# Two attention branches in halves of the array, and two layer boundaries rearranged, in a three-layer fp32 kernel

## The reference

```
first block:  h = rms_norm(x)*w;  proj = h @ w_in
              o_a = g0*o_cmp + g1*o_slc + g2*o_win     # 8 heads of 64 in 2 key-value groups;
                                                       # compressed, selected and window branch
              o_r = group_norm(retention(q, k, v)) * silu(g_ret)     # 4 heads
              x = x + (gate_a*(o_a@w_a) + gate_b*(o_r@w_b)) @ w_mix_out
              x = x + (silu(u_gate)*u_val) @ w_ffn_down              # u: a convolution of h@w_up
              x = rms_norm(x) * norm_final_w
two layers:   u = rms_norm(h)*g;  proj = u @ w_in_2
              h = h + (g_a*(y_a@..) + g_b*(y_b@..) + g_c*(y_c@..)) @ w_o   # pool, conv, attention
              h = h + square(relu(rms_norm(h)*g @ w_up)) @ w_down
              h = h + sigmoid(rms_norm(h)*g @ w_ple_gate) * (p @ w_ple_proj)
```

## Time and profile before

| | |
|---|---|
| median of 3 runs | 2753.8 us (2752.64 to 2756.29) |
| the profiled execution | 2755.44 us, of which 2753.6 us are the span of the trace |
| granted TensorE clock, mean | 0.99 |
| PE busy | 2650.4 us |
| DVE busy | 1557.2 us |
| POOL busy | 1543.7 us |
| ACT busy | 799.0 us |

### The profile page before, as it was taken

The page is one execution under the profiler, slowest core; times in us unless marked ns, Lnnn a source line. Parts: engine busy times, 40 slices in busy tenths (PEclk is TensorE's granted clock), DMA queues, the critical chain, the costliest instruction groups (busy, mean ns, idle before and its releaser), DMA issues.

```text
span 2753.6 us, 35262 instructions
## 1 busy us (share of the span) xinstructions
PE 2650.4 (96%) x11835; PEld 2119.2 (77%) x11835; DVE 1557.2 (57%) x2170; ACT 799.0 (29%) x1178; POOL 1543.7 (56%) x1834
## 2 busy tenths in 40 slices
PE   7899999999999979899999999998989999999999
PEld 5677667888888867668888888887667888888887
DVE  6556665357574767881258233564886236643275
ACT  2332333323222234333222112124333222112112
POOL 5733433666665664345566555675335556665566
PEclk9999999999999989999999999999999999999999
DMA  4311111322222222122222232232112222222223
GB/s 164 123 47 48 44 35 60 133 94 87 102 99 94 91 83 92 46 85 92 94 96 100 93 106 91 91 109 97 62 62 80 96 92 99 101 92 97 101 92 123
DMA packets 36823, 247.26 MB, mean 90 GB/s; under 512 B 4464, under 2 KB 4848, under 8 KB 7792
## 3 DMA queue, kind: packets, MB, share of 16 engines
q1 hardware_dynamic: 34704, 238.57, 24.5%
q10 hardware_dynamic: 2016, 7.35, 0.8%
HBM read 243.81 MB, written 2.10 MB: 89 GB/s over the span
## 4 chain that ended last, share of the span: by engine, by line
PE 37%; POOL 30%; issue 26%; DVE 6%; ACT 1%; POOLq 1%; DMA 0%; DVEq 0%; ACTq 0%; SPq 0%
POOL w_lo L319 30%; PE bank L638 6%; PE bank L640 6%; PE bank L639 6%; PE both L638 4%; PE both L640 4%; PE both L639 4%; PE both L804 1%; PE both L805 1%; PE bank L792 1%; PE bank L825 1%; ACT prob L469 1%; DVE small L1238 1%; PE bank L671 1%; PE bank L827 0%
## 5 line engine op out<-in xcount | busy, mean ns | idle before, releaser
L319 POOL TENSOR_TENSOR w_lo<-raw,w_hi 128x256 fp32r<-128x256 f32 x1788 | 1482.3, 860 | 1119.6 <-ACT w_hi L388 1113.6
L388 ACT ACTIVATE w_hi<-raw 128x1024 fp32r<-128x1024 f32 x446 | 469.1, 1057 | 1031.7 <-PE both L640 501.4
L638 PE MATMUL bank<-a_hi,w_hi 128*128 128x512 f32 x1369 | 559.9, 409 | 0.0
L640 PE MATMUL bank<-a_hi,w_lo 128*128 128x512 f32 x1369 | 536.4, 392 | 0.0
L639 PE MATMUL bank<-a_lo,w_hi 128*128 128x512 f32 x1369 | 535.5, 391 | 0.0
L638 PE MATMUL both<-a_hi,w_hi 128*128 128x512 f32 x864 | 348.5, 403 | 28.8 <-DVE a_lo L1546 19.3
L639 PE MATMUL both<-a_lo,w_hi 128*128 128x512 f32 x864 | 338.8, 392 | 0.0
L640 PE MATMUL both<-a_hi,w_lo 128*128 128x512 f32 x864 | 338.7, 392 | 0.0
L638 PEld LDWEIGHTS bank<-a_hi,w_hi 128*128 128x128 f32 x1369 | 258.9, 189 | 62.2 <-issue 11.0
L639 PEld LDWEIGHTS bank<-a_lo,w_hi 128*128 128x128 f32 x1369 | 258.9, 189 | 56.9 <-issue 6.7
L640 PEld LDWEIGHTS bank<-a_hi,w_lo 128*128 128x128 f32 x1369 | 258.2, 189 | 55.7
(11 more groups left out here) (272 smaller groups left out, 3055.7 us busy)
## 6 DMA issues: line engine op xcount, KB each, us to landing
raw<-stream SPq DMA_DIRECT2D x223, 1024.0 KB, 4.7
h<-xT SPq DMA_DIRECT2D x8, 256.0 KB, 6.3
h<-xT ACTq DMA_DIRECT2D x1, 2048.0 KB, 7.5
outT<-h SPq DMA_DIRECT2D x8, 256.0 KB, 2.3
h<-decay ACTq DMA_DIRECT2D x1, 1024.0 KB, 4.8
h<-rope ACTq DMA_DIRECT2D x1, 1024.0 KB, 6.9
prob<-pT ACTq DMA_DIRECT2D x2, 512.0 KB, 3.5
par<-par ACTq DMA_DIRECT2D x2, 408.0 KB, 3.1
```

What stands on the lines that cost most here:

```text
L319: pool.tensor_tensor(w_lo[:, s, part], raw[:, s, part], w_hi[:, s, part], ALU.subtract).then_inc(lo_done, 1)
L388: act.activation(w_hi[:, s, cols], raw[:, s, cols], ACT.Copy).then_inc(hi_done, 1)
L638: pe.matmul(dst, w_hi[:, s, cols], rhs_hi(k), start=start and k == 0, stop=False)
L640: ins = pe.matmul(dst, w_lo[:, s, cols], rhs_hi(k), start=False, stop=stop and k == nk - 1)
```

## The change

**Heads.** The keys of a group's selected and window branch are now stacked in one tile, 64 partitions each (`k_sw[g]`), and so are the values along their free dimension (`v_sw[g]`); the host reorders the weights for that. The two big score matmuls then use the two row halves of the array; the half that isn't the group's own reads a copy of the query with its partitions exchanged (`q_turned`), which DVE writes in two instructions more per head. The values of the selected branch go to output partitions 0 to 63 and those of the window branch to 64 to 127. The compressed branch shares the first half and is padded to 128 rows. `attention_out` now runs once per group: it copies one half, adds the other, rounds, and subtracts, four instructions on 64 partitions in place of two per head on 128.

**Block to first layer.** The operand of the first layer is made from the unnormed `h` with the product of both gains (`start_gain`), tile by tile, while the last down-projection runs (`start_tile`, `operand_lo`). With f the final gain, the two norms together are one factor, 1/sqrt(mean(x²(f² + eps)) + eps²), so the squares are scaled by sqrt(f² + eps) (`start_root`). The normed `h` itself is made later, between the gate units of the first layer (`late_norm`), with a `square_sum` and a root of its own.

**Layer to layer.** PE raises `operand_read` as it reads each tile in the last gate unit, and ACT and DVE write the next layer's operand behind it. The first two units of both layers run together, with k = 7 of both at the end. DVE adds the squares in place of POOL, and `square_sum` is moved into the third unit. The loops over layers and over the three branches are written out.

```diff
@@ heads: scores and values on PE @@
-                    pe.matmul(b_s0[:, 0:n], q, ks[rows, 0:n], start=True, stop=True)
-                    pe.matmul(b_s1[:, 0:n], q, kw[rows, 0:n], start=True, stop=True)\
-                        .then_inc(scores_ready, score.up())
+                    for half, dst in enumerate((b_s0, b_s1)):
+                        at = slice(half * DH, (half + 1) * DH)
+                        ins = pe.matmul(dst[:, 0:n], (q_turned if half != g else qt)[at, cols],
+                                        k_sw[g][at, 0:n], start=True, stop=True)
+                    ins.then_inc(scores_ready, score.up())
...
-                    if j == 0:
+                    if i == 0:
                         pe.wait_ge(attention_out_read, ofree.due())
-                    pe.matmul(b_o[rows, col], vc[0:NCMP, rows], ptc[0:NCMP, :], start=True, stop=False,
+                    pe.matmul(b_o[0:DH, col], vc[:, g * DH:(g + 1) * DH], ptc, start=True, stop=False,
                               skip_group_check=True)
                     for a in range(i + 1):
-                        pe.matmul(b_o[rows, col], vs[:, a, rows], pt[:, 0, a * P:(a + 1) * P],
-                                  start=False, stop=False, skip_group_check=True)
-                        ins = pe.matmul(b_o[rows, col], vw[:, a, rows], pt[:, 1, a * P:(a + 1) * P],
-                                        start=False, stop=a == i, skip_group_check=True)
+                        for half in range(2):
+                            rows = slice(half * DH, (half + 1) * DH)
+                            ins = pe.matmul(b_o[rows, col], v_sw[g][:, a, rows], pt[:, half, a * P:(a + 1) * P],
+                                            start=half == 1 and a == 0, stop=a == i, skip_group_check=True)
@@ heads: DVE @@
+                q = row_tile(m, t + 3)
+                for g in range(KVG):
+                    V.tensor_copy(q_turned[g * DH:(g + 1) * DH, :], q[(1 - g) * DH:(2 - g) * DH, :])\
+                        .then_inc(vector_step, steps.up())
...
+            def attention_out(t, g):
+                rows = slice(g * DH, (g + 1) * DH)
+                low, out_rows = tile_a[0:DH, :], tile_a[rows, :]
+                V.wait_ge(values_added, pv.due(4))
+                V.tensor_copy(low, b_o[DH:P, :]).then_inc(vector_step, steps.up())
...
+                V.tensor_tensor(out_rows, b_o[0:DH, :], low, ALU.add)\
...
+                hi = row_tile(y_hi, t + 8)[rows, :]
+                V.tensor_copy(hi, out_rows).then_inc(vector_step, steps.up())
...
+                V.tensor_tensor(row_tile(y_lo, t + 8)[rows, :], out_rows, hi, ALU.subtract)\
+                    .then_inc(attention_out_rounded, rounded.up())
...
                 if last is not None and j == 0:
-                    attention_out(last)
+                    attention_out(last, 1)
+                if j == 4:
+                    attention_out(t, 0)
@@ block to first layer: ACT, DVE @@
+            def start_tile(n):
+                act.wait_ge(evac, U_L - KD + n + 5)
+                operand_hi(n, start_gain[:, n:n + 1])
+                square(n, start_root[:, n:n + 1])
...
+                for j in range(8):
+                    ahead(u, j)
+                    if u + 8 == U_L and j > 0:
+                        start_tile(j - 1)
...
                 for n in range(KD):
                     residual(u, n, n)
-                    if tile0 == FT:
-                        square_tile(n, n == KD - 1)
+                    if tile0 == FT and n > 0:
+                        operand_lo(0, n - 1, start_gain[:, n - 1:n])
+                        add_square(0, n - 1)
...
-            rms()
-            for k in range(KD):
-                V.scalar_tensor_tensor(out=h[:, k, :], in0=h[:, k, :],
-                                       scalar=par[:, C1_FIN + k:C1_FIN + k + 1],
-                                       in1=rstd[:, :], op0=ALU.mult, op1=ALU.mult)\
-                    .then_inc(h_tile_ready, 1)
@@ DVE, between the gate units of the first layer @@
+                def late_norm(n):
+                    if n < KD:
+                        square_tile(n, n == KD - 1)
+                    elif n == 15:
+                        V.wait_ge(root_ready, root.due())
+                    if 15 <= n < 17:
+                        cols = slice((n - 15) * S // 2, (n - 14) * S // 2)
+                        V.reciprocal(ssum[:, cols], ssum[:, cols]).then_inc(vector_step, steps.up())
...
+                    if 17 <= n < 21:
+                        for k in (2 * n - 34, 2 * n - 33):
+                            V.scalar_tensor_tensor(out=h[:, k, :], in0=h[:, k, :],
+                                                   scalar=final_gain[:, k:k + 1], in1=ssum[:, :],
+                                                   op0=ALU.mult, op1=ALU.mult)\
@@ layer to layer: ACT @@
+            def next_operand(layer, k):
+                if k < KD - 1:
+                    act.wait_ge(operand_read, (layer - 1) * (KD - 1) + k + 1)
+                else:
+                    act.wait_ge(unit_done, U_L + layer * L_UNITS + 4)
+                act.wait_ge(h_tile_ready, (layer - 1) * KD + k + 1)
+                operand_hi(k, mix_gain[:, layer * KD + k:layer * KD + k + 1])
...
+                    if j == 11 and layer + 1 < LAYERS:
+                        for k in range(KD - 1):
+                            next_operand(layer + 1, k)
@@ layer to layer: DVE @@
                 for n in range(KD):
+                    follows = n == KD - 1 and layer + 1 < LAYERS
+                    if follows:
+                        for k in range(KD - 2):
+                            next_lo(k)
                     scaled((tile_a, tile_b)[n % 2], bank4(n), ul + L_PLE + 4, n)
+                    if follows:
+                        next_lo(KD - 2)
                     ple_out(n)
+                    if follows:
+                        next_lo(KD - 1)
+                if layer + 1 < LAYERS:
+                    for k in range(KD):
+                        add_square(layer + 1, k)
@@ start of a layer: PE @@
-            with repeat(pe, LAYERS, [...]) as layer:
+            for layer in range(LAYERS):
...
-                for j in range(4):
-                    unit(ul, j, 4, [bank4(j)], a_op(), 8, next_a if j == 0 else None)
-                    if j == 1:
-                        square_sum()
+                together(ul, 2, 1, a_op(), 8, next_a)
+                for j in range(2, 4):
+                    unit(ul, j, 4, [bank4(j)], a_op(), 8,
+                         lambda k: square_sum() if (j, k) == (2, 2) else None)
```

More of the change, by code:

```diff
@@ L641, in product, with unit @@
                                     stop=stop and k == nk - 1)
+                    if read is not None and k < nk - 1:
+                        ins.then_inc(read, 1)
                 return ins
-            def unit(u0, j, lag, dsts, rhs, nk, first=None, start=True, stop=True):
+            def unit(u0, j, lag, dsts, rhs, nk, first=None, start=True, stop=True, read=None):
                 s, cols = conv_unit_slot(j)
@@ L1022, in _ @@
                             unit(ub, half * 6 + j, [2, 3, 3, 4][j], [bank4(j)], a_op(), 8)
+                            if (layer, br, half, j) == (0, 1, 0, 1):
+                                square_sum()
                         if half == 0:
@@ L1044, in _ @@
                         square_sum()
-                singles(ul + L_PLE + 4, 8, a_op(), first=next_a, lags=first_lags)
+                singles(ul + L_PLE + 4, 8, a_op(), first=next_a, lags=first_lags,
+                        read=operand_read if layer + 1 < LAYERS else None)
         @block.vector
@@ L1473, in _, with operand_lo, add_square @@
             rms()
+            def operand_lo(layer, k, gain):
+                V.wait_ge(hi_tile_ready, layer * KD + k + 1)
+                V.scalar_tensor_tensor(out=a_lo[:, k, :], in0=h[:, k, :], scalar=gain, in1=a_hi[:, k, :],
+                                       op0=ALU.mult, op1=ALU.subtract).then_inc(a_tile_ready, a_rdy.up())
+            def add_square(layer, k):
+                if k == 0:
+                    return
+                V.wait_ge(x_square_ready, (layer + 1) * KD + k + 1)
+                V.wait_ge(vector_step, steps.now())
+                ins = V.tensor_tensor(ssum[:, :], m[:, 0, :] if k == 1 else ssum[:, :], m[:, k, :], ALU.add)
+                if k == KD - 1:
+                    ins.then_inc(squares_ready, sums.up())
+                    V.wait_ge(squares_ready, sums.now())
+                else:
+                    ins.then_inc(vector_step, steps.up())
             V.memset(ssum[:, 0:1], 0.0).then_inc(vector_step, 1)
@@ L1759, in _ @@
                             scaled(work[:, j * S:(j + 1) * S], bank4(j), ub, half * 6 + j)
+                            if layer == 0:
+                                late_norm(br * 8 + half * 4 + j)
                         V.wait_ge(activated, res.due(4))
```

165 lines of the change are left out of this document (76 added, 89 removed).

## The result

The changed kernel took 2710.8 us (median of 4 runs, 2709.8 to 2712.9) and the one before 2753.2 on the same chip, a ratio of 0.9845, with a 95% interval of 0.9828 to 0.9862. The forecast was 2710. The profiled execution took 2711.0 us, with a span of 2709.2.

A forecast was written before the change was run, and what follows sets the result against it. The prediction took PE, busy 96% of the span, as the bound. Heads 16.5, block to first layer 18.5 and layer to layer 9.0 sum to 44.0 us off 2753.8, giving 2709.8, say 2710; range 2700 to 2729.

The forecast's parts named there:

- Boundary 1: From the block to the first layer: third unit starts sooner without a stall; 18.5 us gained, bounds 14 and 19.4.
- Boundary 2: From the first layer to the second: third unit starts sooner without a stall; 9.0 us gained, bounds 6 and 9.9.
- the allowance of 0.9: Layer to layer: 0.9 us taken off the 9.9 for thin margins of operand tiles, squares and weights.
- Scores and values in halves: Heads, steps 3 to 6: shorter score pairs and values on PE gain all, 4.9 us a head.
- the rule on its drain: Heads, compressed branch: changing tiling mode drains the array, changing tile does not; without it the sum is 4 us less.
- Steps 0 to 2: Heads 2 to 4: `attention_out`'s four DVE instructions take about 3.2 us, step 1's mask starts about 1.1 us later.
- Step 7: End of a head: chain starts 0.83 us sooner, two query copies of 0.43 enter it; gain 0.4 us.
- about 1.4 of steps 0 to 2: First head, which has no output to take: its steps 0 to 2 gain about 1.4 us.
- the term of the clock: Heads: longer waits at step 2 leave PE more at the lower clock; 1.5 us lost over three heads.
- Heads bound by DVE: Rival: the heads stay bound by DVE and give 5 us, so 2721 us; chance 1 in 10.
- Operands late: Rival, at the boundaries: waits replace part of the stalls, 10 us less gain, 2720 us; chance 1 in 10.
- Slower instruction fetch: Rival: written-out loops make PE fetch new code in the second layer, time about 2798 us; chance 1 in 20.

The follow-up runs named there:

- Experiment 1: The kernel before with the change in the heads alone, both boundaries and the loops as before; 2740.6 against 2755.4 us, ratio 0.9947.
- Experiment 4: The changed kernel with the first layer's operand made only behind the last down unit, still without the norm; ratio 0.9858.
- Experiment 5: The changed kernel with the second layer's operand made only behind the last gate unit; ratio 0.9856.
- experiment 2: The changed kernel with selected and window values both in output partitions 0 to 63, the compressed branch alone in 64 to 127; ratio 0.9857.
- experiment 3: The changed kernel with both score products of a step in the upper row half, the window's keys left out; ratio 0.9866.
- Experiments 7: The changed kernel with POOL's last subtraction of a head issued as four instructions of 128x256; ratio 0.9822, 2704.0 us.
- experiment 8: The changed kernel with the window half copied twice in the second group's `attention_out`, one more DVE instruction; ratio 0.9853.
- Experiment 6: The changed kernel with DVE's next query copies in slot 7 behind the sum of squares, not at the slot's head; ratio 0.9859.
- experiment 10: The changed kernel with POOL's last subtraction in four instructions and the first head's query copies ahead of the compression; ratio 0.9809, 2701.7 us.

## Why the prediction was right, step by step

**Boundary 1** (18.5, measured 20.1). The mechanism was right, with no new wait: DVE's `a_lo` of k = 6 and 7 ended 977.6 and 979.9, early enough. The size was 0.5 short because a `square_sum`'s 0.9 us was counted whole ahead of the third unit. The timeline at 987.76 above shows that only 0.46 lies before the next matmul and 0.4 behind it. The remaining 1 us comes in the layer itself: one of PE's waits for a head norm fell from 1.29 to 0.53, and the attention steps took some 0.15 us less each, about 1 us in all, of which a lower clock took 0.8 back. Experiment 1, where the loops over layers stand as before, shows neither, and experiments 4 and 5 show both. That points to the loops written out, whose only effect the prediction had seen as a risk; no run took them alone. The third unit's weights, which ACT rounds late, delayed nothing: 10.88 us lie between the first matmul of the two units and that of the third, the free pace. Experiment 4 adds what the prediction did not ask: had the operand stayed behind the units, 17.5 of 20.4 would still have come.

**Boundary 2** (9.0, measured 9.7 at the third unit, 10.3 by the end). The thin margins were real, and they cost 0.17 and 0.37 us of waiting; the allowance of 0.9 was about right and the `square_sum` count erred the same way as above. From the third unit on the gain first fell to 8.6, with a wait of 0.28 at the fifth unit, and then rose by 1.7 in the layer, by the same shorter waits as in the first. Experiment 5 shows that the early place was needed here, and that 3 us of the old stall lay in front of ACT's first `a_hi`, which the prediction's sum removed without naming them.

**Scores and values in halves.** Forecast: 4.9 us for steps 3 to 6 of every head. Measured from the scores of step 3 to those of step 7: 4.81, 4.83, 4.95 and 4.85. The largest term of the heads was therefore exact, and experiments 2 and 3 show each half of its mechanism. One sign was missed: the pair of scores was to take 1.0 to 1.1 us and took 1.26, because the compressed scores run in between; with these counted the saving is 0.86, forecast 0.83. The distance of 0.36 us that followed the compressed matmul of 31 rows is gone: values of four key tiles save 1.01 us, forecast 1.03. No run changed the mode by itself, so the rule on its drain stays as the rows left it.

**Steps 0 to 2** (-1.1 a head, measured -1.1, -1.7, -1.1). `attention_out` grew from 1.69 to 2.83 us, not to 3.2, and still step 1's mask came 1.1 later, measured from its scores (1.39 to 2.45 us). Experiments 7 and 8 support both links: DVE at step 0, then the long POOL instruction at step 2. The Trainium skill's exclusive lock (SBUF — State Buffer, Who interferes with whom) agrees with them: 1.94 us behind a long POOL instruction, 0.33 behind a quarter of it, for an instruction that takes 0.25 alone. The wait at step 2 came to 5.07, as forecast (5 to 6). Of the waits announced for steps 0, 1 and 7, those at 1 and 7 came and the one at 0 didn't.

**Step 7** (0.4 in each of three heads, measured 1.0, -0.4, 0.3). The sum was right and its account was only half right. The end of the maxima to the end of the probabilities grew by 1.5 us (3.80 to 5.3). The copies are 0.5 of it: 0.88 us of DVE, of which 0.4 fall into what was a wait for ACT, as the prediction said. The other 1.0 it lacked: the probabilities' instructions now begin as POOL's next `w_lo` does, in the first head:

```profile
189.58 3.15 POOL L322 TENSOR_TENSOR w_lo<-raw,w_hi 128x256 fp32r<-128x256 f32 x4 [10.56 <-ACT w_hi L374]
```

```profile
189.54 1.06 DVE L1298 TENSOR_SCALAR prob<-prob,small 128x512 f32<-128x512 f32 x1
190.52 0.70 DVE L1301 TENSOR_SCALAR work<-work,small 128x31 f32<-128x31 f32 x1
```

Before, the same two took 0.54 and 0.23 us. PE reached the transposes 0.6 us later relative to the scores, and got it back from values that are 1 us shorter. (The 1.0 has a slower clock before in it, the -0.4 one after; 0.3 is the head without either.) Experiment 6 shows that the place which it tried for the copies is worse.

**Where the heads fell short** (16.5 forecast, 14.2 measured with the clock behind them). Two of its steps failed. The first is the first head's gain of "about 1.4 of steps 0 to 2", which was 0.0. PE now waits 2.40 us for the first query's `td` (before 1.1), and the first scores come 1.07 us later, about as allowed for. Then PE stays longer at the lower clock. From the first scores to those of step 1, PE has the same 33 matmuls in both kernels:

```profile
116.24:125.86 9.62, 9.62 (x33) 7.40 (x33) 2.88 (x12) 3.54 (x11) 5.45 (x8) 0.67 0.38 124
```

Before, from 115.17 to 123.63, they took 8.46 us at a mean clock of 0.80. That is 1.2 us, and the term of the clock had counted only the later heads. But the late query doesn't by itself bring this about. In experiment 2, after a wait of 2.39 us for the same `td`, the same matmuls took 8.24 us:

```profile
116.45:124.69 8.24, 8.24 (x33) 6.40 (x33) 2.92 (x12) 3.56 (x11) 5.47 (x8) 0.79 0.33 127
```

There, and in experiment 8 with a wait of 2.83, the first head's steps 0 to 2 gained the 1.4 that was forecast, just as with the copies early (experiment 10). So the term was there, and the changed kernel's profiled execution lost as much to the clock; why the clock stays low longer in some executions is open.

The second is that no clock was counted behind the last head, where 1.5 us were lost. PE waits 3.19 us for `y_lo`; the first matmul behind it takes 0.59 us to the next instead of 0.33, and six more go at 0.43 us instead of 0.23:

```profile
460.76 0.80 PE L645 MATMUL both<-y_hi,w_hi 128*128 128x512 f32 x1 [3.19 <-DVE y_lo L1352]
461.36 0.63 PE L646 MATMUL both<-y_lo,w_hi 128*128 128x512 f32 x1
```

Before, a wait of 1.6 us at that place cost no clock. The length of the wait is not the whole of it, though. In experiment 3 PE waits as long there, and the pace behind is 0.24 us:

```profile
470.58 0.50 PE L645 MATMUL both<-y_hi,w_hi 128*128 128x512 f32 x1 [3.20 <-DVE y_lo L1352]
470.92 0.40 PE L646 MATMUL both<-y_lo,w_hi 128*128 128x512 f32 x1
```

Inside the three later heads the term of 1.5 for the clock shows as 0.6, in the third: its steps 0 to 2 lost 1.7 where the others lost 1.1.

**The rivals.** "Heads bound by DVE" would have given 5 and gave 15.7: steps 3 to 6 had the room that the prediction read from their slack. "Operands late" fell with the waits of 0.5 us in all. Slower instruction fetch fell with the pace: 0.227 us per matmul in the feed-forward as before and 0.227 in the second layer; the loop that was written out had itself cost time, 2.5 us of ACT's at its turn (experiment 5). The errors went both ways, 2.3 us too much on the heads and 2.9 too little on the boundaries. That they cancel is luck, so the total is closer than the terms deserve; by the medians it was 1.6 us too high (44.0 against 42.4).

## What to carry to other kernels

Work that is taken off the bounding engine pays in full where the chain behind it has slack, and that slack is read step by step from the timeline, not from shares of busy time. A small DVE instruction on the path should not lie beside a long POOL instruction: cutting POOL's 2.3 us instruction in four cost POOL 0.5 us and gave the kernel about 6, of which the shorter waits are 4.8. At the boundary with a norm between two matmul stages, taking it out of the operand (scaling later) was worth far more than preparing the operand earlier; at the boundary without one the earlier place was half of the gain. What an edit does beside its purpose should be looked for: here the loop written out most likely took a table load and an idle stretch of ACT off the path.

## What was new about the hardware

Two matmuls in the two column halves, or the two row halves, ran beside each other with nothing in the program but their order: starts 0.02 us apart, and each half's own line (five matmuls or eight) set the time. At the same place a wait of PE of 1.6 us left the clock at the upper of its two levels and one of 3.2 us was followed by six matmuls at the lower (0.43 us apart instead of 0.23), but not in every execution: in experiment 3 the clock stayed up behind 3.20 us. ACT's sequencer took 2.5 us from the branch of the long loop over the layers to its next instruction (0.2 at the short loop over the branches), and a table load of 1.28 us stood behind it; with the loop written out both were gone. DVE's 128x512 copy took 0.43 us alone and 2.00 us beside POOL. Cut in four, POOL's subtraction let such instructions through between its parts.
